# Start addresses of the operand tiles in SBUF: from odd offsets to whole 2 KB rows

## The reference, cut to what matters

```python
proj = jnp.einsum("bsd,de->bse", h, w_in[l])            # 1024 x 1024 by 1024 x 5280
y_sb = jnp.einsum("bsc,cd->bsd", o_sb * silu(gate_sb), w_o_sb[l])
x = x + jnp.einsum("bsd,de->bse", merged, w_out[l])
...
proj = h @ w_in[l]                                      # 1024 x 1024 by 1024 x 7168
x = x + (g_a * y_a + g_b * y_b) @ w_out[l]
gt, up = jnp.split(h @ w_gate_up[l], 2, axis=-1)        # 1024 x 1024 by 1024 x 5632
x = x + (jax.nn.silu(gt) * up) @ w_down[l]
```

## The kernel before

| tile | side | remainder |
|---|---|---|
| `ident`, then `mask` (1,024 B), `ones` (512 B), `eps`, `lam`, `vectors` (1,360 B) | left | 128, 640, 1664, 128, 160, 192 |
| `w_raw`, `w_hi`, `w_lo` | left | 1568 |
| `s_` up to `s_left`, `cq`, `ckv`, `k`, `m_t`, `f_y`, `g_late`, `r_late`, `d_q`, `d_k`, `d_v`, `d_t`, `d_probs`, `attn`, `ff` (all a multiple of 2,048 B long) | left | 1568 |
| `s_probs` (behind `s_left`, 8,200 B long) | left | 1600 |
| `d_group_ones` | left | 1632 |
| `h_hi`, `h_lo` of each of the three norms (32 KB each) | right | 2016 |

## Time and profile before

### The profile page before, as it was taken

One profiled execution on the slowest core, in us unless ns is written; L12 is line 12 of the kernel. 1 busy time (PEld: TensorE's weight loads), 2 busy tenths in 40 slices (PEclk: granted clock), 3 DMA queues, 4 the chain that ended last, 5 costly groups with the idle time before them and its releaser, 6 DMA issues. The chain is left out here.

```text
span 3138.9 us, 34002 instructions
## 1 busy us (share of the span) xinstructions
PE 2884.7 (92%) x13392; PEld 2336.5 (74%) x13392; DVE 1582.0 (50%) x1942; ACT 1231.3 (39%) x2019; POOL 727.1 (23%) x322
## 2 busy tenths in 40 slices
PE   3999999887878888999999999979989999999999
PEld 2878888666766766777777777758877888888887
DVE  3465665136785343788888876746432121111121
ACT  3454554134562243555566556545224110111110
POOL 1111111111001231333332332314223222222221
PEclk6999999998999999999999999989999999999999
DMA  4111122203213421212212122145430111111112
GB/s 106 41 48 50 48 66 73 68 19 67 63 41 128 144 85 51 78 44 64 68 56 62 56 67 63 68 150 170 156 107 27 47 48 47 47 47 47 48 47 81
DMA packets 239286, 219.16 MB, mean 70 GB/s; under 512 B 29304, under 2 KB 200856, under 8 KB 239128
## 3 DMA queue, kind: packets, MB, share of 16 engines
q1 hardware_dynamic: 238096, 215.41, 22.4%
q10 hardware_dynamic: 1032, 1.57, 0.4%
HBM read 156.66 MB, written 41.42 MB: 63 GB/s over the span
## 5 line engine op out<-in xcount | busy, mean ns | idle before, releaser
L179 POOL TENSOR_TENSOR w_lo<-w_raw,w_hi 128x1024 fp32r<-128x1024 f32 (+3 forms) x220 | 515.9, 2347 | 1890.3 <-ACT w_hi L171 1890.2
L171 ACT ACTIVATE w_hi<-w_raw 128x1024 fp32r<-128x1024 f32 (+3 forms) x220 | 215.5, 983 | 600.4 <-PE f_banks L239 203.1
L2227 DVE SCALAR_TENSOR_TENSOR d_acc<-d_padded,vectors,d_acc 128x1024 f32<-128x1024 f32 x240 | 389.6, 1623 | 3.0
L209 PE MATMUL d_pp<-h_hi,w_hi 128*128 128x512 f32 x896 | 362.9, 405 | 9.5 <-PEq L67 4.5
L209 PE MATMUL d_pp<-h_hi,w_lo 128*128 128x512 f32 x896 | 363.5, 406 | 0.0
L209 PE MATMUL d_pp<-h_lo,w_hi 128*128 128x512 f32 x896 | 360.7, 403 | 0.0
L239 PE MATMUL f_banks<-h_hi,w_hi 128*128 128x512 f32 x704 | 222.0, 396 | 4.5 <-PEq L67 4.5
L239 PE MATMUL f_banks<-h_lo,w_hi 128*128 128x512 f32 x704 | 221.8, 396 | 0.0
L239 PE MATMUL f_banks<-h_hi,w_lo 128*128 128x512 f32 x704 | 221.5, 395 | 0.0
L209 PE MATMUL s_pp<-h_hi,w_hi 128*128 128x512 f32 x512 | 206.3, 403 | 10.6 <-PEq L67 10.6
L2006 POOL TENSOR_TENSOR d_probs<-d_probs 128x128 f32<-128x128 f32 (+3 forms) x64 | 133.5, 2086 | 340.2 <-ACT d_probs L2122 340.2
(11 more groups left out here) (338 smaller groups left out, 5818.7 us busy)
## 6 DMA issues: line engine op xcount, KB each, us to landing
w_raw<-in_w_in SPq DMA_DIRECT2D x97, 512.0 KB, 3.9
w_raw<-in_w_gate_up SPq DMA_DIRECT2D x44, 512.0 KB, 3.8
w_raw<-in_w_down SPq DMA_DIRECT2D x22, 512.0 KB, 3.6
gates<-s_gate SPq DMA_DIRECT2D x16, 512.0 KB, 5.0
f_gate<-gates SPq DMA_DIRECT2D x16, 512.0 KB, 4.8
w_raw<-in_w_out SPq DMA_DIRECT2D x16, 512.0 KB, 3.8
w_raw<-in_w_proj SPq DMA_DIRECT2D x16, 512.0 KB, 5.1
x_tok_in<-in_x SPq DMA_DIRECT2D x8, 512.0 KB, 12.1
```

Of the source, the lines that this page charges most:

```text
L171: act.activation(self.hi[:, s, 0:chunks, :], self.raw[:, s, 0:chunks, :], ACT.Copy).then_inc(self.rounded[s], 1)
L179: pool.tensor_tensor(self.lo[:, s, 0:chunks, :], self.raw[:, s, 0:chunks, :], f32(self.hi[:, s, 0:chunks, :]), ALU.subtract).then_inc(self ...
L209: mm = pe.matmul(halves(ps)[h], w[:, k, :], x[:, k, h * HALF:(h + 1) * HALF], start=(k == 0 and r == 0), stop=(k == chunks - 1 and r == 2))
L2227: dve.scalar_tensor_tensor(out=acc[:, :], in0=x, scalar=wt, in1=acc[:, :], op0=ALU.mult, op1=ALU.add).then_inc(c["taps"], 1)
```

## The change

Three constant tiles (`eps`, `lam`, `vectors`) and the mask move to the right side, ahead of everything else there. Of the two masks, only the first is loaded and kept. Two tiles that nothing reads or writes fill up: `row_start` of 896 bytes on the left, behind `ident` and `ones`, and `row_end` of 64 bytes on the right. No instruction is added or taken away, but for the DMA of the mask, which brings 64 KB instead of 128 KB.

```diff
+ROW_START, ROW_END = 224, 16
...
-            sp.dma_start(mask[:, :, :], a["masks"].rearrange("n p k -> p n k")).then_inc(mask_loaded, 16)
+            sp.dma_start(mask[:, :], a["masks"][0]).then_inc(mask_loaded, 16)
...
         ident = mem.sb("ident", [P, P])
-        mask = mem.sb("mask", [P, 2, P])
         ones = mem.sb("ones", [P, P])
-        eps = mem.sb("eps", [P, 1])
-        lam = mem.sb("lam", [P, 1])
-        vectors = mem.sb("vectors", [P, width])
+        mem.sb("row_start", [P, ROW_START])
         ring = WeightRing(mem)
+        vectors = mem.sb("vectors", [P, width], side="right")
+        mask = mem.sb("mask", [P, P], side="right")
+        eps = mem.sb("eps", [P, 1], side="right")
+        lam = mem.sb("lam", [P, 1], side="right")
+        mem.sb("row_end", [P, ROW_END], side="right")
...
-                               mask[:, 0, :], one_part(KC, a["w_in"], C_CQ, C_CQ + P))
+                               mask[:, :], one_part(KC, a["w_in"], C_CQ, C_CQ + P))
```

## The result

The changed kernel takes **3111.5 us** (median of 4 runs, 3110.9 to 3111.7) against 3139.0 us (4 runs, 3135.1 to 3141.7) for the kernel before: a ratio of 0.9907, 95% interval 0.9892 to 0.9921. The profiled span falls from 3138.9 to 3109.9 us, by 29.0. The prediction said 2996, with a range from 2965 to 3105: the direction is right, the gain is a fifth of the one forecast, and the time lies 6 us above the range.

What follows compares the result with a forecast made beforehand. TensorE was taken as the bound. Stage savings of 47.8 + 26.2 + 40.2 + 9.1 + 10.5 + 4.2 + 2.6 = 140.6 us took the span from 3138.9 to 2998.3, timed 2996 us; range 2965 to 3105.

Steps and rivals of the forecast that it cites:

- What bounds the kernel: Whole kernel: TensorE, busy 92% of the span, so what one product takes sets most of the time.
- Starts of the moving operands: All stages: moving starts go from 2016 and 1568 to 0, a product falls to 216 ns; 140.6 us saved.
- the slower case: Rival, 3202 us, chance 0.07: equal starts make moving read and weight load meet, 240 ns a product.
- The half-rate rows: Products at half clock or unsplit float32: 430 ns, 3 ns beyond their columns; at full rate taken as 216 ns.
- Stationary starts, "nothing more is added": Line 1634: stationary `h` at 2016 instead of 1568 costs 2.2 ns, already inside the other prices.
- Narrow products of 256 columns: Stick-breaking, differential and latent attention: 119.3 ns each, 9.6 ns of it to be saved.
- The shares credited: Part of each stage's saving expected to arrive: feed-forward in full, stick-breaking nine tenths, differential eight, latent attention four.
- the rival on weight loads: Rival, 3094 us, chance 0.12: loads of the next stationary operand keep 226.7 ns; only `h`'s 6.6 ns go, 42.7 us.
- what is late next: Differential stage: VectorE's share rises from 82% to 86%, so eight tenths of 50.2 us are credited, 40.2.
- VectorE, ScalarE, GpSimd, mask: Moved operands cost these engines 0; the mask's halved DMA gains 0 to 2 us, taken as 0.
- It does nothing: Rival, 3136 us, chance 0.13: the 6.6 ns come from `h`'s half of SBUF or the fp32r type, not the start.
- 16-byte lines: Skill page on SBUF: accesses pay per line crossed, so starts at multiples of 32 bytes cost the same; sum 0.

Runs made afterwards that it cites:

- the run with the light VectorE: 240 convolution instructions (line 2227) cut to 128 of 1024 columns, once in the kernel before (3084.0 us), once in the changed kernel (3054.4 us).
- everything at 96: Changed kernel with fillings resized so that left operand tiles and `h` all start at 96 instead of 0: 3107.8 us.

## Why the prediction was wrong

*What bounds the kernel*: right. TensorE's products set the time, no instruction was added or taken away, and the time moved by what a product takes. The line with moving `h` was the dear one, and it moved.

*Starts of the moving operands*: this is the step that failed, in the sentence "I take 216 ... a whole row is the shortest that the supply can be". No row of before showed a start at 0; what I had was two starts with two prices, and I read the price off the moving operand's address alone. The rows allowed the other reading: in both 226.7 ns cases the two operands had the same remainder, and in the 233.3 ns case they didn't; I even wrote the first half of that down, against the slower case. The price of distance 0 was thus already in the rows: every product whose two operands stood at 1568 was at its best before the change, and the term for it should have been 0. In the feed-forward it was 47.8 us forecast and 13.7 measured; 2112 x 6.6 = 13.9 is what the moving `h` alone gives.

The half-rate rows, at 3 ns above their columns, led me to take the whole 10.7 ns as supply that can be mended. They show only that the cost vanishes at half rate. No layout of this study got below 226.7.

*Stationary starts, "nothing more is added"*: wrong in kind. The 2.2 ns of line 1634 was the price of a distance (64), not of a stationary start; it fell to about 227 ns, and this is all that line 1634 had to give.

*Narrow products of 256 columns*: forecast 9.6 ns less than 119.3; in the trace after the median from start to start is still 120.

*The shares credited*: too generous as well, and for a reason that isn't only waits. With the right price (the rival on weight loads used it, for another reason) they give 42.7 us, and 29.0 came. The feed-forward hit (14.1 against 13.7). The differential stage was to give 14.3 and gave 6.3, stick-breaking 9.2 and 5.7. The price came from unbroken runs, and these two stages mix the projection with other work. From start to start of neighbouring projection products (those under 300 ns apart) the mean fell from 233.8 to 229.3 ns in stick-breaking and from 233.7 to 228.7 in the differential stage, by 4.5 and 5.0 and not by 6.6; from the eighth pair of an unbroken run on it fell by 6.0 in the latter (233.3 to 227.3). So TensorE's busy time fell by 6.2 us in stick-breaking, where 1536 x 6.6 is 10.1, and by 11.0 in the differential stage, where 2688 x 6.6 is 17.7; why the first products after other work stay dearer wasn't tried. The waits then took 0.6 us and 4.7 us. In stick-breaking the credit for waits, nine tenths, was right; in the differential stage, where TensorE's share fell from 93.9 to 93.3%, under six tenths of what the products saved arrived (6.3 of 11.0), not eight. VectorE, in the prediction "what is late next", holds some 4 us of it by the run with the light VectorE, not all.

*VectorE, ScalarE, GpSimd, mask*: right. Line 2228 took 1627 ns on the mean (1623 before), and SyncE's wait for the mask fell from 4.6 to 3.5 us without a trace in the sum.

*The rivals*: the products came out as in "the weight loads take it", at 174 us for 768, but its reason isn't shown, so the hit is luck: with a smaller load the product got longer. "It does nothing" was right that a start by itself is worth nothing (everything at 96 is as good as at 0). By the Trainium skill's 16-byte lines ("SBUF — State Buffer", DMA port swizzle), weighed in the prediction, all these layouts would be equal; the runs differ by 6.6 ns a product on whole lines. The Trainium skill's page "TensorE: Matmul & The Clock Gate" (Part 2, step by step) gives TensorE two independent read ports, one for the streaming operand and one for the weights. This case's trace speaks against full independence: the price depends on how the two addresses stand to each other, from 226.7 to 234.3 ns. Where in the chip the two meet, no run here shows.

## What to carry to other kernels

Where wide full-rate fp32r products run back to back, as here, look at the start of the moving operand less the start of the stationary one: if it is no multiple of 256 bytes, a small filling tile may be worth up to 3% of a product's time (6.6 of 233 ns here, 4.5 to 5.0 where other work stood between the products). A pitch (the time from one start to the next) from unbroken runs tells two layouts apart to about a tenth of a nanosecond, but an operation's price can hang on each of its operands: before one address is credited, tabulate all of them. And don't take a bare rate for a price that can be reached when no row shows it.

## What was not expected of the hardware

- The price of a full-rate product repeats with 256 bytes of distance: 226.7 ns at 0 and 256, 228.9 at 64, 232.4 to 234.3 at every other multiple of 32, and it isn't symmetric (64 costs 228.9, 192 costs 233.3).
- Products with fewer stationary columns took longer, though their loads were shorter: 226.7 ns in a row at 128 columns, 229.8 at 64, 232.0 at 32. What it hangs on wasn't tried.
- After two pauses of the same length (2.99 and 2.97 us) in the same place of the program the granted clock was 1.00 once and 0.50 the other time; the stage got 2.2 us longer for it, in place of 0.4 shorter as in a run with the changed layout that kept its clock (121.4 us). So the layout alone doesn't decide it; what does wasn't tried.
